# First tile's rows weighted and turned block by block in a two-layer decoder step, its root mean square as a factor, and weights laid out in 8 KB runs

## The reference

```python
def rmsnorm(x, w):
    xf = xf * lax.rsqrt(jnp.mean(xf * xf, axis=-1, keepdims=True) + EPS)
    return (xf * w.astype(jnp.float32)).astype(x.dtype)
def peer(h, wq, keys, u, v):            # h = rmsnorm(x, norm_ffn)
        q = (tb @ wq).reshape(blk, PEER_HEADS, PEER_D_KEY)
        s1 = jnp.einsum('thd,hkd->thk', q[..., :half], keys[:, 0])
        s2 = jnp.einsum('thd,hkd->thk', q[..., half:], keys[:, 1])
        sc1, i1 = lax.top_k(s1, PEER_TOPK)
        sc2, i2 = lax.top_k(s2, PEER_TOPK)
        # the best 16 of 16 x 16 sums choose idx
        act = jax.nn.gelu(jnp.einsum('thkd,td->thk', u[idx], tb), approximate=False)
        wgt = (g * act.astype(jnp.float32)).astype(tb.dtype)
        return jnp.einsum('thk,thkd->td', wgt, v[idx])
x = x + (ga * ya + gb * yb) @ w_out
x = x + peer(rmsnorm(x, norm_ffn), peer_wq, peer_keys, peer_u, peer_v)
```

## Time and profile before

| what | us |
|---|---|
| median of 3 runs (2141.39 to 2147.22) | 2143.99 |
| the profiled execution's own time | 2136.45 |
| its span, first to last instruction | 2134.9 |
| first layer: first gather issued | 384.03 |
| second layer: first gather issued | 1442.39 |

### The profile page before, as it was taken

One profiled execution on the slowest core, in us unless ns is written; L12 is line 12 of the kernel. 1 busy time (PEld: TensorE's weight loads), 2 busy tenths in 40 slices (PEclk: granted clock), 3 DMA queues, 4 the chain that ended last, 5 costly groups with the idle time before them and its releaser, 6 DMA issues. The chain is left out here.

```text
span 2134.9 us, 30025 instructions
## 1 busy us (share of the span) xinstructions
PE 1668.2 (78%) x10874; PEld 846.6 (40%) x10874; DVE 1449.6 (68%) x3604; ACT 489.0 (23%) x1411; POOL 671.0 (31%) x614
## 2 busy tenths in 40 slices
PE   7998899877786666766689988998787776666666
PEld 6877667533332111111168875674232331111111
DVE  3555543878778878877726555447887888787786
ACT  2245311311121221111222542113112112111112
POOL 0011000444444454444300110004444444444442
PEclk9999999987887676566899999999778877656668
DMA  6468797899999999999955678969999999999997
GB/s 202 156 200 300 240 370 259 362 411 421 415 416 421 413 417 420 417 416 413 368 163 162 217 275 277 378 239 390 414 420 414 420 419 406 422 421 419 413 416 312
DMA packets 187648, 749.04 MB, mean 351 GB/s; under 512 B 16611, under 2 KB 74444, under 8 KB 116434
## 3 DMA queue, kind: packets, MB, share of 16 engines
q0 software_dynamic: 84640, 588.54, 67.4%
q1 hardware_dynamic: 102850, 158.48, 21.8%
HBM read 735.63 MB, written 11.52 MB: 350 GB/s over the span
## 5 line engine op out<-in xcount | busy, mean ns | idle before, releaser
L1215 PE MATMUL ps<-arena 64*64 64x512 f32 x4096 | 747.6, 830 | 383.2 <-DVE arena L1803 381.8
L2426 POOL DMA_INDIRECT arena<-in_peer_uv,arena x528 | 623.4, 1181 | 781.3 <-PE ps L1215 634.3
L1794 DVE CUSTOM_DVE_ANT_0 arena<-arena,h 128x1024 f32<-128x1024 f32 x512 | 627.3, 1225 | 252.5 <-DMA arena<-in_peer_uv,arena 246.4
L1215 PEld LDWEIGHTS ps<-arena 64*64 64x64 f32 x4096 | 141.1, 165 | 936.0 <-DVE arena L1803 887.8
L569 PE MATMUL ps<-ht_tok,wring 128*128 128x264 f32 (+1 forms) x1536 | 369.5, 399 | 14.4 <-DMA wring<-in_w_in 13.1
L569 PEld LDWEIGHTS ps<-ht_tok,wring 128*128 128x128 f32 x1536 | 296.4, 196 | 87.9 <-issue 18.6
L2165 ACT ACTIVATE arena<-arena 128x1 f32<-128x1 f32 x528 | 106.0, 203 | 973.8 <-DVE arena L1794 972.5
L1803 DVE TENSOR_SCALAR arena<-consts,arena 128x64 f32<-128x64 f32 (+1 forms) x528 | 164.2, 311 | 11.4 <-ACT arena L2165 10.8
L569 PE MATMUL ps<-arena,wring 128*128 128x264 f32 x256 | 63.9, 393 | 3.9 <-DVE arena L1522 3.9
L2405 POOL DMA_DIRECT2D nrow<-in_norm_ffn x2 | 1.1, 534 | 187.8 <-PE ps L919 187.8
L569 PE MATMUL ps<-arena,gate 128*128 128x256 f32 x256 | 59.0, 382 | 0.0
(11 more groups left out here) (366 smaller groups left out, 1783.0 us busy)
## 6 DMA issues: line engine op xcount, KB each, us to landing
arena<-in_pages SPq DMA_DIRECT2D x256, 272.0 KB, 5.0
wring<-in_w_in SPq DMA_DIRECT2D x38, 1024.0 KB, 5.6
arena<-in_peer_uv,arena POOLq DMA_INDIRECT x528, 12.8
h<-in_state_ssm POOLq DMA_DIRECT2D x16, 512.0 KB, 6.9
out<-h POOLq DMA_DIRECT2D x16, 512.0 KB, 6.5
wring<-in_w_ssm_proj SPq DMA_DIRECT2D x8, 1024.0 KB, 7.9
arena<-in_w_out SPq DMA_DIRECT2D x8, 1024.0 KB, 9.2
wring<-in_peer_wq SPq DMA_DIRECT2D x8, 1024.0 KB, 9.6
```

Source lines behind the costliest of these rows:

```text
L1215: last = pe.matmul(ps[to:to + 64, SUM_BANK[t] + i, :], diag[rows, n % DIAGS, 0:64], ring[rows, HOME[n % RING], cols], start=n in TILE_FIRS ...
L1794: dve.tensor_tensor_reduce(ring[:, HOME[k], 0:D_MODEL], ring[:, HOME[k], 0:D_MODEL], tokens, 1.0, 0.0, ALU.mult, ALU.add, dots[:, column(n ...
L2426: pool.indirect_dma_start(ring[:, HOME[k], :], None, table, bass.IndirectOffsetOnAxis(ap=idx[:, TOPK * u + j:TOPK * u + j + 1], axis=0)).t ...
```

## The change

For tile 0, DVE writes each block of 256 columns, as it is added to `x`, also multiplied by the norm's weights but not by the root mean square (`first_out`), and PE turns its two chunks at once (`first_rows`). The root mean square, now computed beside the products, is a factor in the copy of tile 0's scores and in its gelus. The queries' weights of head 0 are in `wq_home` and their chunks interleave (`first_queries`). The mix of the samples and all their later steps stand behind the first scores, and the second tile's `out` is spread between them. DVE finishes the first eight experts of the first unit before the second eight (`first_eight`), takes the dot products of slots 0 and 1 early, and postpones `sample_gated`. POOL's waits follow: slot 4 still waits for `out_samples(0)`, slot 6 now for `out_samples(1)`, slot 7 for `out(3, 1)`. The second tile of head 0 is asked and scored at slots 28 to 32, not at the end. All weight blocks are laid out on the host so that each partition's part of a block is one run of 8 KB (5 to 8 KB for the tail).

```diff
-    for hh, begun in ((0, LATE_HEADS), (1, LATE_HEADS + 8)):
-        steps[begun] = [("queries", hh, 0, P, TOKENS)]
-        steps[begun + 3] = [("queries", hh, 1, P, TOKENS)]
-        steps[begun + 6] = [("scores", hh, (1,))]
+    for hh, at in ((0, FIRST_HEAD_AGAIN), (1, (LATE_HEADS, LATE_HEADS + 3, LATE_HEADS + 6))):
+        steps[at[0]] = [("queries", hh, 0, P, TOKENS)]
+        steps[at[1]] = [("queries", hh, 1, P, TOKENS)]
+        steps[at[2]] = [("scores", hh, (1,))]
     for half in range(2):
...
             if hh == 0:
-                pe.wait_ge(sem("latents_load"), 16)
-                state["wq", hh] = wq_latents
+                pe.wait_ge(sem("home_load"), 16)
+                state["wq", hh] = wq_home
...
-    rows_of = lambda t, c: hp[t].rearrange("p (q c) -> p c q", c=DC)[:, c, :]
+    rows_of = lambda t, c: hp[t][:, c * P:(c + 1) * P]
...
+    def first_rows(k):
+        pe.wait_ge(sem("aux_free"), 4 + marks["out", k, 0])
+        b = aux.fill()
+        for e in range(2):
+            last = turn(ps[:, b, e * P:(e + 1) * P], rows_of(0, 2 * k + e), P)
+        aux.filled(last)
+        marks["rows", k] = aux.n
+    def first_queries(m, chunks, banks):
+        for c in chunks:
+            if c % 2 == 0:
+                pe.wait_ge(sem("aux_free"), 4 + marks["rows", c // 2])
+            last = pe.matmul(ps[:, banks[m], 0:P], wq_home[:, c, m * P:(m + 1) * P], ht[:, c, 0:P], start=c == 0, stop=c == DC - 1)
+        return last
     pe.wait_ge(sem("mixed"), 1)
     out(0, 0)
     pe.wait_ge(sem("sample_weights"), 1)
     b = aux.fill()
     aux.filled(turn(ps[:, b, 0:SAMPLES], fin[0:SAMPLES, 384:512], SAMPLES))
     out(1, 0)
+    first_rows(0)
+    out(2, 0)
+    first_rows(1)
+    out(3, 0)
+    marks["x", 0] = aux.n
+    first_rows(2)
+    pe.wait_ge(sem("home_load"), 16)
+    state["wq", 0] = wq_home
+    banks = (wide.fill(), wide.fill(ahead=1))
+    first_queries(0, range(0, 4), banks)
+    first_rows(3)
+    first_queries(1, range(0, 4), banks)
+    for m in range(2):
+        wide.filled(first_queries(m, range(4, DC), banks))
+    marks["q", 0] = wide.n
+    scores(0, (0,))
...
-    out(2, 0)
+    out(0, 1)
     pe.wait_ge(sem("wide_free"), 4 + marks["samples_mixed"])
     b = wide.fill()
     for k in range(4):
         last = turn(ps[:, b, k * P:(k + 1) * P], smix[:, k * P:(k + 1) * P], P)
     wide.filled(last)
     marks["mixed", 1] = wide.n
-    out(3, 0)
-    marks["x", 0] = aux.n
+    out(1, 1)
     sample_heads()
     sample_mla_parts()
-    pe.wait_ge(sem("ph_ready"), 1)
-    for q in range(2):
-        b = aux.fill()
-        for c in range(4 * q, 4 * q + 4):
-            last = turn(ps[:, b, (c % 4) * P:(c % 4 + 1) * P], rows_of(0, c), P)
-        aux.filled(last)
-    marks["turned", 0] = aux.n
-    pe.wait_ge(sem("aux_free"), 4 + marks["turned", 0])
-    queries(0, 0, 0, P)
-    queries(0, 1, 0, P)
-    scores(0, (0,))
+    out(2, 1)
     queries(1, 0, 0, P)
+    queries(1, 1, 0, P)
     sample_mla()
-    queries(1, 1, 0, P)
-    out(0, 1)
     scores(1, (0,))
-    out(1, 1)
     pe.wait_ge(sem("mixed"), 2)
     out_samples(0)
     out_samples(1)
-    out(2, 1)
+    out(3, 1)
     pe.wait_ge(sem("aux_free"), 4 + marks["sums"])
     for half in range(2):
         b = aux.fill()
         aux.filled(pe.matmul(ps[0:SAMPLES, b, :], cst("sel8"), hp[2][:, half * 512:(half + 1) * 512], start=True, stop=True))
-    out(3, 1)
     marks["x", 1] = aux.n
...
-    out(0, 0)
+    def first_out(k):
+        cols = slice(k * BLOCK, (k + 1) * BLOCK)
+        b = aux.read()
+        then(dve.tensor_tensor(x[:, 0, cols], x[:, 0, cols], ps[:, b, 0:BLOCK], ALU.add))
+        aux.emptied(dve.tensor_tensor(hp[0][:, cols], x[:, 0, cols], nrow[:, cols], ALU.mult))
+    def first_rows(k):
+        b = aux.read()
+        aux.emptied(dve.tensor_copy(ht[:, 2 * k:2 * k + 2, 0:P], ps[:, b, 0:BLOCK].rearrange("p (c t) -> p c t", c=2)))
+    dve.wait_ge(sem("ffn_row_load"), 16)
+    first_out(0)
     b = aux.read()
     aux.emptied(dve.tensor_tensor(f_wd[:, :, 0:A_HEADS], bc(ps[:, b, 0:SAMPLES], 2, A_HEADS), bc(cst("sel8"), 1, SAMPLES), ALU.mult), wait=True)
     dve.nop().then_inc(sem("sample_mix"), 1)
-    for k in range(1, 4):
-        out(k, 0)
+    first_out(1)
+    first_rows(0)
+    first_out(2)
+    first_rows(1)
+    first_out(3)
+    first_rows(2)
+    first_rows(3)
     px_mean(0, slice(45, 46))
-    dve.wait_ge(sem("ffn_row_load"), 16)
-    px_rows((0,))
-    for q in range(2):
-        b = aux.read()
-        aux.emptied(dve.tensor_copy(ht[:, 4 * q:4 * q + 4, 0:P], ps[:, b, :].rearrange("p (c t) -> p c t", c=4)))
+    dve.wait_ge(sem("px0_root"), 1)
+    dve.reciprocal(st[:, 51:52], st[:, 48:49]).then_inc(sem("ph_ready"), 1)
...
+    def first_eight(k):
+        eight = slice(8 * k, 8 * k + 8)
+        split = lambda ap: ap.rearrange("p (s i) -> p s i", s=2)[:, :, eight]
+        dve.tensor_scalar(iw[:, 8 * k:8 * k + 8], ctopi[:, eight], 4, None, ALU.logical_shift_right)
+        then(dve.tensor_scalar(iw[:, TOPK + 8 * k:TOPK + 8 * k + 8], ctopi[:, eight], 15, None, ALU.bitwise_and))
+        then(dve.tensor_copy(split(sel), split(iw)))
+        picks = hot[:, 256:512].rearrange("p (s i j) -> p s i j", s=2, j=TOPK)
+        then(dve.tensor_tensor(picks, bc(split(sel), 3, TOPK), bc(bc(cst("iota"), 1, 8), 1, 2), ALU.is_equal))
+        then(dve.tensor_tensor(picks, picks, bc(topf.rearrange("p (s j) -> p s j", s=2), 2, 8), ALU.mult))
+        then(dve.tensor_reduce(split(sel), picks, AX.X, ALU.add))
+        dve.scalar_tensor_tensor(out=idx[:, 8 * k:8 * k + 8], in0=sel[:, 8 * k:8 * k + 8], scalar=float(N_KEYS),
+                                 in1=sel[:, TOPK + 8 * k:TOPK + 8 * k + 8], op0=ALU.mult, op1=ALU.add).then_inc(sem("idx_ready"), 1)
     def best_experts(u):
...
             yield
+            if u == 0:
+                first_eight(k)
             if k == 0:
...
     for _ in best_experts(0):
         pass
+    out(0, 1)
+    out(1, 1)
+    inputs(0)
+    out(2, 1)
+    inputs(1)
     sample_gated()
-    out(0, 1)
     ahead = best_experts(1)
     for _ in range(10):
         next(ahead)
-    out(1, 1)
     for half in range(2):
         copy4(hp[2][:, half * 512:(half + 1) * 512])
     def late_tiles(n):
-        if n == 1:
-            out(2, 1)
-        elif n == 2:
+        if n == 0:
+            out(3, 1)
+        elif n == 1:
             for half in range(2):
...
+    act.wait_ge(sem("aux_free"), 4 + marks["x", 0])
+    squares(peer("sc")[:, 0:D_MODEL], x[:, 0, :], st[:, 45:46], "px0_squares")
+    root(st[:, 48:49], st[:, 45:46], "px0")
...
+        if (hh, tiles[0]) == (0, 0):
+            act.wait_ge(sem("ph_ready"), 1)
+        for t in tiles:
+            dst, src = keysc[:, hh, t, :, :].rearrange("p s n -> p (s n)"), ps[:, b, 2 * P * t:2 * P * (t + 1)]
+            last = act.activation(dst, src, ACT.Copy, scale=st[:, 51:52]) if t == 0 else act.copy(dst, src)
+        scored_bank(last)
...
+        norm = st[:, 51:52] if UNITS[u][0] == 0 else 1.0
+        act.activation(gel[:, at:at + 1], dots[:, at:at + 1], ACT.Gelu, scale=norm).then_inc(sem("gelu_ready"), 1)
...
-    w_in = of_layer("w_in", layer).rearrange("(p c) n -> p c n", c=DC)
-    w_ssm = of_layer("w_ssm_proj", layer).rearrange("(c p) n -> p c n", p=P)
-    w_out = of_layer("w_out", layer).rearrange("(c p) n -> p c n", p=P)
-    w_mla = of_layer("w_mla_proj", layer).rearrange("(c p) n -> p c n", p=P)
+    w_in, w_ssm, w_out, w_mla = (of_layer(name, layer).rearrange("k p (c n) -> k p c n", c=chunks) for name, chunks in (
+        ("w_in", DC), ("w_ssm_proj", DC), ("w_out", DC), ("w_mla_proj", 4)))
     def tail_block(n):
-        first, cols = TAIL[n]
-        load_block(w_in[:, :, C_DT + first:C_DT + first + cols], DC, cols)
+        load_block(of_layer(f"w_tail{n}", layer).rearrange("p (c n) -> p c n", c=DC), DC, TAIL[n][1])
     def block_of(w, first, k):
-        load_block(w[:, :, first + k * BLOCK:first + (k + 1) * BLOCK], DC, BLOCK)
+        load_block(w[first // BLOCK + k], DC, BLOCK)
...
-    sp.dma_start(wq_home, w_q[4]).then_inc(sem("home_load"), 16)
+    sp.dma_start(wq_home, w_q[0]).then_inc(sem("home_load"), 16)
     sp.wait_ge(sem("lat_stores"), 64)
     sp.wait_ge(sem("wide_full"), marks["samples_mixed"])
-    sp.dma_start(wq_latents, w_q[0]).then_inc(sem("latents_load"), 16)
+    sp.dma_start(wq_latents, w_q[4]).then_inc(sem("latents_load"), 16)
...
-        if j == 0:
-            pool.wait_ge(sem("idx_ready"), u + 1)
+        if n in (0, TOPK // 2):
+            pool.wait_ge(sem("idx_ready"), 1 + n // (TOPK // 2))
+        elif j == 0:
+            pool.wait_ge(sem("idx_ready"), u + 2)
         if n == 3:
             pool.wait_ge(sem("wide_full"), marks["heads", 2])
         elif n == 4:
             pool.wait_ge(sem("aux_full"), marks["sums", 0])
-        elif n in (6, 7):
-            pool.wait_ge(sem("aux_full"), marks["out", n - 4, 1])
+        elif n == 6:
```

(11 more changed lines are left out.)

51 lines of the change are left out of this document (24 added, 27 removed).

## The result

The changed kernel takes 2163.5 us, median of 5 runs, against 2144.0: a ratio of **1.0090, interval 1.0070 to 1.0111**. It is 19.5 us slower, and lies 11 us above the forecast's range. Its profiled execution has a span of 2161.9 us (2134.9 before).

A forecast was written before the change was run, and what follows sets the result against it. Gathers were taken as bound by DMA bytes, and PE as the bound elsewhere, losing time to late weights. Terms -13.5 and +8.4 sum to -5.1 us, forecasting 2138.9 from a median of 2143.99; range 2126 to 2152.5.

The forecast's parts named there:

- The 8 KB runs: Gate's last weight blocks: 8 KB runs land sooner, in 7.5 us, cutting PE's waits; 13.5 us gained over both layers.
- 1 us of stall for each of the two blocks: PE's remaining wait at each of the gate's two late weight blocks; 1.9 us a layer in all.
- rival 3: Gate's blocks land no sooner, delayed by surrounding states and pages; only the 8.4 us loss remains, 2152.4 us; chance 0.15.
- its mark of 9.5 us: Gate's block landing time above which the blocks' gain would be smaller than the bridge's loss.
- The first tile's chain: Bridge: root mean square off the chain, scores and choice sooner; first gather issued at 373.9, 10.1 us sooner.
- Loads behind the mix: Bridge: four query-weight loads issued at 379.4, among gathers, cost 10 us and give back the 10.1 but for 0.3 us.
- slot 4 at 398.0: Slot 4's gather, waiting for `out_samples(0)`, issued at 398.0; DMA engines dry from 395.7, 4.5 us lost a layer.
- a stall of 5.8 us: PE at head 1's queries waits for the load of `wq_spare`, landing after 9.2 us, at 388.6.
- The price of all that: Bridge: 4.5 us lost less 0.3 gained, 4.2 a layer; 8.4 us for two, between 0 and 11.
- slots 4 to 7 keep the engines busy until 410: Gather stage: first `outputs` at about 406 instead of 400.13 cost nothing more.
- Rival 1: Query weights land in time because engines serve SP's queue first; gain 13.5 + 0.6, 2129.9 us; chance 0.18.
- rival 2: Earlier gathers count in full, 10.1 us twice, as if the loads found room; 2110.3 us; chance 0.07.

The follow-up runs named there:

- the runs alone: Kernel before the change with only the projection weights laid out in 8 KB runs: 2139.1 us, ratio 0.9971.
- the sums first: Changed kernel with the samples' last steps before head 1's queries and DVE copying the sums before unit 1's choice: 2165.6 us, ratio 1.0098.
- both choices first: Changed kernel, head 1's and 4's loads swapped, mix earlier, head 1's queries and scores behind head 0's, DVE choosing for both units early: 2149.1 us, ratio 1.0021.
- The filler: Six extra matmuls on PE ahead of outputs of slots 4, 5, 6; ratio 0.9977 on the samples' steps early, 0.9983 on the runs alone, 0.9997 on head 1's block first.
- the samples' steps early: Changed kernel with the samples' mix, turns, heads and parts ahead of head 0's queries again, their other steps in the old order: 2143.8 us, ratio 0.9999.
- head 1's block first: Changed kernel with two weight loads swapped, head 1's into the place SP fills first, head 4's into the later one: 2146.8 us, ratio 1.0010.
- the loads late: The samples' steps early with only SP's query-weight loads for heads 1 to 5 held back: 2172.1 us, ratio 1.0118.

## Why the prediction was wrong, step by step

**The 8 KB runs, -13.5 us: mis-sized, -4.4 by the medians and -6.2 by the ratio.** The failed sentence is "In 8 KB runs I keep the number of packets' turns (104 to 259)". The run with the runs alone had 14 turns to 221 in the same place and 102 to 36 in the 3 us after it. "1 us of stall for each of the two blocks" became 2.5 each, and the waits of both layers stayed at 13.0 us for 13.2. The DMA share there is 1.0 from 180 to 200. That a landing is set by all that lies in the queues, as rival 3 said, fits this and is not shown by itself; its mark of 9.5 us lies between the two landings, 9.0 and 10.6 us.

By the rule of the Trainium skill that the prediction named (DMA: Bandwidth & Descriptors, Specifications: line rate from 512 B on) the term is 0. The ratio 0.9971 (0.9954 to 0.9988) shuts out both 0 and 13.5 us and lies about half way, and the 305 and 358 GB/s of busy engine speak against the rule too. Of its rule on turns by the packet (Queues, rings and completion order) the 14 to 221 show no even share either, though no run shows that the packets which the profile counts are the page's.

**The first tile's chain, first gather 10.1 us sooner: right.** It came 11.4 us sooner, 10.7 against `out(0, 0)`. The root is off the chain, and its factor in gelu costs nothing that shows (0.9999 with it, 0.9996 without).

**Loads behind the mix, 10 us given back but for 0.3; slot 4 at 398.0; a stall of 5.8 us: the times right, to about a microsecond.** SP's load was due at 379.4 and went at 378.37; the wait was 5.80, slot 4 at 397.78. The DMA share before it was 0.58 from 390 to 400, 4.2 us of hole for the 4.5. Three small sums of the prediction are off and change nothing: the load's time adds up to 379.2 and slot 4's to 397.8, and half of the blocks' gain above 2138.9 ends at 2145.7, not 2147.

**The price of all that, 8.4 us for both layers: wrong, and the larger part of the miss.** The bridge with all that follows costs 1.0090 less 0.9971, 25.5 us. So 17.1 of the 24.6 us between forecast and measurement lie here and 7.3 in the runs' term, and either by itself would have turned the sign. The sentence that failed is "slots 4 to 7 keep the engines busy until 410, so that costs nothing more". The prediction priced a wait of PE by the DMA time that runs dry ahead of one gather. The kernel with the sums first took that dry time away and won nothing (1.0098). The prediction listed what queues behind the stall: `sample_mla`, `scores(1)`, the sums, the outputs. It did not follow `scores(1)` one engine further, to DVE. There stands the choice for unit 1, some 9 us of work. The kernel before begins it at 384.39 and does the larger part, 5.6 us, before it has a slot's dot to take. In the changed kernel DVE stood 11.59 us behind PE, began the choice at 396.05, and everything that DVE had behind it came late: the sums' copies, the first diagonal (403.72 for 394.34) and the dots of slots 2 to 7, by 7.6 to 10 us. In both kernels the last steps of the choice stand between dots, ending at 408.27 and 415.89. With that PE ran out of work (3.98 of 10 us in 410 to 420), its clock fell, and the rows, queries and outputs behind went at 1.2 GHz for much of the time. By this the gathers, though bound by bytes elsewhere, had holes, the largest of those behind 400 in the windows 3.7 us between 460 and 470.

What of this is shown and what is read: that the wait for one block carries 17 us is shown, by two loads changed over and by the loads held back. The way by DVE is read from the timelines. The run with both choices first took the late choice away and gained nothing over the exchange of the loads, so the choice is one link of the way and not the cause. The filler bears on PE's clock in two other orders: with the samples' steps early its gain stands at the edge of the intervals, beside a control without gain, and with head 1's block first it is only suggested.

In sizes, by the ratios: 17 us are the wait for head 1's block with what hangs on it (5.8 us of wait, 8.5 us of time per layer; in the run with the loads late 12.24 and 12.8). The clock is 4.7 us where the samples' steps stand early, and 2.8 with head 1's block first. About 6 us of 25.5 stay open, and each of these sizes has an interval of some 4 to 6 us either way.

**The rivals.** Rival 3 had the right sign and 0.15 of the chances, for half of the right reason: its blocks gained little, but its 8.4 us for the bridge were a third of the 25.5. Rival 1 (the loads land in time) and rival 2 (earlier gathers count in full) are out. The range failed because both its ends for the bridge, 0 and 11 us, were ends of the same dry time; no case priced what DVE does late behind PE's wait, or PE's clock behind that.

## What to carry to other kernels

When a step is moved, ask for each engine which work it does now while others still prepare, and whether a new wait pushes that work into a full stage; a wait can cost more than its own length there, here 8.5 us for 5.8. Two loads of the same size are not the same: the block wanted first goes to the place that comes free first, and this single exchange was worth 17 us. Where an engine's granted clock falls in a stage that it nearly bounds, added work of no use can be faster than idling, and a control in a version whose clock is up helps to tell whether that was the reason.

## What the runs showed of the hardware that was not expected

- Packets of 7 KB on SP's queue beside state copies on POOL's queue got 14 turns to 221 in the first 3 us and 102 to 36 in the next. Packets of 1 KB had 104 to 259, and in the first 3 us the bytes were much the same (0.10 and 0.13 MB). The share of a queue changes within a few us.
- Weight blocks in runs of 8 KB moved 358 GB/s of busy engine where runs of 1 KB moved 305, and one alone landed in 4.8 us instead of 5.5. Among state copies and pages it took 9.0 to 10.6 us.
- Eighteen matmuls of no use in each layer raised the granted clock of 20 us from 0.50 and 0.65 to 1.00 in a program of 2144 us that ran 4.7 us faster with them. On a kernel whose slots were quick already they gained nothing (0.9983 against 0.9971).
- A gelu that takes its scale from memory is 294 ns instead of 203, and 256 of them cost nothing that could be measured.
